# Output projection of a transformer block: six weight parts read during the merge, modulation reads spread between the rows, router on four column groups with a summing product

## What is computed

```python
merged = gates[:, :, 0] * y_pool + gates[:, :, 1] * y_conv + gates[:, :, 2] * y_mla
y = jnp.matmul(merged, w_out)                      # 1024x1024 by 1024x1024
...
h = layer_norm(DEEPNORM_ALPHA * h + y, ln1_g, ln1_b)
...
aff = jax.nn.sigmoid(jnp.matmul(xt, w_router))     # xt is h, w_router is 1024x16
```

## Time and profile before

| | |
|---|---|
| runs | median 3368.93 us of 3 (3367.58 to 3374.35) |
| profiled execution | 3366.2 us, span 3364.5 us |
| busy share of the span | PE 88%, PEld 68%, DVE 61%, ACT 43%, POOL 14% |
| mean granted TensorE clock | 0.936 of full speed |

### The profile page before, as it was taken

How to read it: one execution, slowest core, us unless ns; L and a number is a source line. 1 busy time by engine, 2 the same in 40 slices (tenths; PEclk the granted TensorE clock), 3 DMA queues, 4 the chain that set the end, 5 groups by cost and what they waited for, 6 DMA issues and landing times. The chain is left out here.

```text
span 3364.5 us, 37190 instructions
## 1 busy us (share of the span) xinstructions
PE 2973.2 (88%) x13692; PEld 2296.3 (68%) x13692; DVE 2062.4 (61%) x1983; ACT 1460.3 (43%) x1547; POOL 480.4 (14%) x495
## 2 busy tenths in 40 slices
PE   5999777999997779999997979998988739999994
PEld 3884455666756648888885757886776637888883
DVE  4997464122125668988885634227762268888885
ACT  3112444111102147787764431115651127777773
POOL 0005300000000001111111201009431100000002
PEclk8999899999998889999998989999998769999997
DMA  6112321010106346995224311100012259999995
GB/s 244 47 34 71 124 57 38 35 69 34 69 15 261 126 196 259 392 415 220 80 76 163 111 68 40 48 19 26 1 77 75 115 216 360 392 400 391 401 383 208
DMA packets 113974, 534.57 MB, mean 159 GB/s; under 512 B 15728, under 2 KB 27760, under 8 KB 74048
## 3 DMA queue, kind: packets, MB, share of 16 engines
q1 hardware_dynamic: 91600, 454.07, 35.1%
q0 software_dynamic: 15840, 57.68, 5.2%
q10 hardware_dynamic: 6416, 21.24, 1.7%
HBM read 561.40 MB, written 65.91 MB: 186 GB/s over the span
## 5 line engine op out<-in xcount | busy, mean ns | idle before, releaser
L1763 DVE TENSOR_TENSOR upper_split<-arena,upper_split 128x2048 fp32r<-128x2048 f32 x186 | 415.2, 2286 | 63.3 <-ACT upper_split L1709 63.3
L3081 DVE TENSOR_TENSOR upper_split_experts<-arena,upper_split_experts 128x2048 fp32r<-128x2048 f32 x144 | 328.9, 2292 | 46.0 <-ACT upper_split_experts L3035 44.7
L1709 ACT ACTIVATE upper_split<-arena 128x2048 fp32r<-128x2048 f32 x186 | 342.6, 1914 | 5.2 <-PE banks L177 3.9
L3035 ACT ACTIVATE upper_split_experts<-arena 128x2048 fp32r<-128x2048 f32 x144 | 275.4, 1918 | 95.5 <-PE banks L177 95.5
L175 PE MATMUL banks<-upper_split_experts 128*128 128x512 f32 x768 | 304.1, 396 | 12.4 <-DVE upper_split_experts L3081 12.4
L175 PE MATMUL banks<-upper_split 128*128 128x512 f32 x744 | 296.9, 399 | 11.7 <-DVE upper_split L1763 11.1
L177 PE MATMUL banks<-upper_split_experts 128*128 128x512 f32 x768 | 301.3, 392 | 0.0
L176 PE MATMUL banks<-upper_split_experts 128*128 128x512 f32 x768 | 301.0, 392 | 0.0
L177 PE MATMUL banks<-upper_split 128*128 128x512 f32 x744 | 291.7, 392 | 0.0
L176 PE MATMUL banks<-upper_split 128*128 128x512 f32 x744 | 291.6, 392 | 0.0
L1134 DVE TENSOR_TENSOR upper_latent<-arena,banks 128x512 f32<-128x512 f32 x48 | 33.0, 687 | 340.6 <-PE banks L1079 339.7
(11 more groups left out here) (442 smaller groups left out, 6244.0 us busy)
## 6 DMA issues: line engine op xcount, KB each, us to landing
arena<-in_exp_up_k SPq DMA_DIRECT2D x124, 1024.0 KB
arena<-in_gate_up SPq DMA_DIRECT2D x96, 1024.0 KB, 8.4
arena<-in_exp_down_k SPq DMA_DIRECT2D x62, 1024.0 KB
arena<-in_down SPq DMA_DIRECT2D x48, 1024.0 KB, 7.3
upper_middle<-in_gate_up SPq DMA_DIRECT2D x32, 1024.0 KB, 8.3
upper_middle<-in_down SPq DMA_DIRECT2D x16, 1024.0 KB, 6.9
y<-arena POOLq DMA_DIRECT2D x31, 512.0 KB, 2.9
arena<-in_merge_w SPq DMA_DIRECT2D x8, 1536.0 KB, 7.6
```

The lines of the kernel that those rows point to most:

```text
L1709: a.activation(rounded(high[s]), raw[s], ACT.Copy).then_inc(high_made[up], 1)
L1763: v.tensor_tensor(rounded(low[s]), raw[s], plain(high[s]), ALU.subtract).then_inc(low_made[up], 1)
L3035: a.activation(rounded(high[n % RING]), raw[n % RAW], ACT.Copy).then_inc(high_made, 1)
L3081: v.tensor_tensor(rounded(low[n % RING]), raw[n % RAW], plain(high[n % RING]), ALU.subtract).then_inc(low_made, 1)
```

## The change

In `merge`, SP issues w_out parts 0 to 2 as soon as step 6's gate weights are split and parts 3 to 5 as soon as step 7's are, ahead of the last two stores. Parts 0 to 5 land where `wg` lies, and parts 6 and 7 land behind it, where `merge` keeps its gate values, so these two are issued in the next block. Each part has a buffer of its own. The four vectors are read over parts 0 to 3, each when its part is split. The four pieces of w_ada go out one at a time behind merged(n) and xhat(n) of n = 2 to 5. The router has the operands swapped: 16 columns of its matrix are stationary and 128 columns of `hT` move; part k writes PSUM partitions 32*(k%4) and up, so that eight matmuls make four partial sums (`partial`), ScalarE copies the 128x128 block (`part`), and one product with a constant 0/1 matrix `pick16` adds the four and turns the result (`logits`). VectorE copies all logits once at the end and no longer after each tile.

The diff, cut to its core (left out are the names of semaphores, the placing of `part_of`, and L1356, which now reads `raw[k]`):

```diff
@@ merge, sync
                 for j in range(2):
                     store(it, j)
                     load(it + 1, j)
+            for j in range(2):
+                sp.wait_ge(low_made, (ND - 1 + j) * NB)
+                for k in range(3 * j, 3 * j + 3):
+                    sp.dma_start(m["wo"][k], core.ins["w_out_k"][:, k, :]).then_inc(m["wo_loaded"][k], 16)
             store(last, 0)
             store(last, 1)
@@ output_and_norm
-    raw = [b[n] for n in ("work", "hT", "h0", "h1")]
+    raw = m["wo"]
@@ output_and_norm, sync
-            def load_w(k):
-                if k >= NW:
-                    sp.wait_ge(w_low, k - NW + 1)
-                sp.dma_start(raw[k % NW], core.ins["w_out_k"][:, k, :]).then_inc(wo_loaded[k % NW], 16)
-
             load_merged(0)
-            for k in range(ND):
-                load_w(k)
-                if k == 3:
-                    load_merged(1)
-                    for dst, name in ((ga, "ln_in_g"), (ba, "ln_in_b")):
-                        sp.dma_start(dst, row_on_all(core.ins[name], D)).then_inc(weights, 16)
-                    load_x(0)
-            for dst, name in ((g1, "ln1_g"), (b1, "ln1_b")):
+            for k in range(6, ND):
+                sp.dma_start(raw[k], core.ins["w_out_k"][:, k, :]).then_inc(wo_loaded[k], 16)
+            load_x(0)
+            load_merged(1)
+            load_x(1)
+            sp.dma_start(wr, core.ins["w_router_k"]).then_inc(weights, 16)
+            for i, (dst, name) in enumerate(((ga, "ln_in_g"), (ba, "ln_in_b"), (g1, "ln1_g"), (b1, "ln1_b"))):
+                sp.wait_ge(w_low, i + 1)
                 sp.dma_start(dst, row_on_all(core.ins[name], D)).then_inc(weights, 16)
-            sp.dma_start(wr, core.ins["w_router_k"]).then_inc(weights, 16)
-            load_x(1)
-            for j in range(4):
-                sp.dma_start(m["ada"][j], core.ins["w_ada"][4 + j]).then_inc(ada_loaded, 16)
             for n in range(2, NT):
                 load_merged(n)
                 load_x(n)
+                if n < 6:
+                    sp.dma_start(m["ada"][n - 2], core.ins["w_ada"][n + 2]).then_inc(ada_loaded, 16)
@@ output_and_norm, tensor
-            def logits(n):
+            def partial(n):
                 pe.wait_ge(weights, 16 * 5)
+                pe.wait_ge(cleared, 1)
                 pe.wait_ge(moved, n + 1)
                 if n:
-                    pe.wait_ge(kept, n)
+                    pe.wait_ge(part_moved, n)
                 for k in range(ND):
-                    t = pe.matmul(ps[:, 4, 0:NE], hT[:, k, :], wr[:, k, :], start=(k == 0), stop=(k == ND - 1))
-                t.then_inc(routed, 1)
+                    q = 32 * (k % 4)
+                    t = pe.matmul(ps[q:q + NE, 4, 0:P], wr[:, k, :], hT[:, k, :],
+                                  start=(k < 4), stop=(k >= 4), skip_group_check=True)
+                t.then_inc(parted, 1)
+
+            def logits(n):
+                pe.wait_ge(part_moved, n + 1)
+                pe.matmul(ps[:, 5, n * NE:(n + 1) * NE], part_of, core.col("pick16"),
+                          start=True, stop=True, skip_group_check=True).then_inc(summed, 1)
 
             product(0)
             for n in range(1, NT):
                 product(n)
+                if n >= 3:
+                    logits(n - 3)
                 if n >= 2:
-                    logits(n - 2)
+                    partial(n - 2)
                 turn(n - 1)
+            logits(NT - 3)
+            partial(NT - 2)
+            turn(NT - 1)
             logits(NT - 2)
-            turn(NT - 1)
+            partial(NT - 1)
             logits(NT - 1)
@@ output_and_norm, scalar
+            def part(n):
+                a.wait_ge(parted, n + 1)
+                if n:
+                    a.wait_ge(summed, n)
+                a.activation(part_of, ps[:, 4, 0:P], ACT.Copy).then_inc(part_moved, 1)
+
...
                 a.wait_ge(h_ready, n + 1)
                 a.dma_start(m["h1"][n], b[f"h{n % 2}"]).then_inc(h_stored[n % 2], 16)
+                if n:
+                    part(n - 1)
                 a.wait_ge(turned, n + 1)
-                if n:
-                    a.wait_ge(routed, n)
                 a.activation(b["hT"], flat2(ps, 2), ACT.Copy).then_inc(moved, 1)
+            part(NT - 1)
@@ output_and_norm, vector
-            def keep(n):
-                v.wait_ge(routed, n + 1)
-                v.tensor_copy(m["logits"][:, n * NE:(n + 1) * NE], ps[:, 4, 0:NE]).then_inc(kept, 1)
-
+            v.memset(ps[:, 4, 0:P], 0.0).then_inc(cleared, 1)
...
             for n in range(NT):
                 norm(n)
-                if n:
-                    keep(n - 1)
-            keep(NT - 1)
+            v.wait_ge(summed, NT)
+            c.did(v.tensor_copy(m["logits"], ps[:, 5, 0:P]))
```

More of the change, by code:

```diff
@@ L70, in _columns @@
         ("lams", 4 * HD2), ("c", 8), ("c_ctx", 8), ("zeros", 32),
-        ("eps_rms", 1), ("eps_ln", 1), ("conv2", 12), ("flip", 128),
+        ("eps_rms", 1), ("eps_ln", 1), ("conv2", 12), ("flip", 128), ("pick16", 16),
     ):
@@ L1172, in output_and_norm @@
     sem = lambda n: core.semaphore("og_" + n)
-    NW = 4
     m_loaded, x_loaded, h_stored = ([sem(f"{n}{i}") for i in range(2)] for n in ("m", "x", "h_stored"))
-    wo_loaded = [sem(f"wo{i}") for i in range(NW)]
-    (weights, made, taken, var_ready, rstd_ready, h_ready, turned, moved, routed, kept, steps, pool_steps,
+    wo_loaded = m["wo_loaded"]
+    (weights, made, taken, var_ready, rstd_ready, h_ready, turned, moved, cleared, parted, part_moved, summed, steps, pool_steps,
      ada_loaded, cols_loaded, w_high, w_low, m_high, m_low, scaled) = map(
-        sem, ("weights", "made", "taken", "var", "rstd", "h_ready", "turned", "moved", "routed", "kept", "steps",
+        sem, ("weights", "made", "taken", "var", "rstd", "h_ready", "turned", "moved", "cleared", "parted", "part_moved", "summed", "steps",
               "pool_steps", "ada", "cols", "w_high", "w_low", "m_high", "m_low", "scaled"))
@@ L1186, in output_and_norm @@
     at = m["st_at"]
+    part_of = core.place(at + 32, P)
     st, mv, rstd = core.place(at, 12), core.place(at + 12, 2), core.place(at + 16, 1)
@@ L1299, in high_m @@
                 a.activation(rounded(fl(mh[j])), b[f"mt{j}"], ACT.Copy).then_inc(m_high, 1)
+            def part(n):
[3 more added lines that the diff above has]
+                a.activation(part_of, ps[:, 4, 0:P], ACT.Copy).then_inc(part_moved, 1)
             high_m(0)
             for k in range(ND):
-                a.wait_ge(wo_loaded[k % NW], 16 * (k // NW + 1))
-                a.activation(rounded(wh[:, k, :]), raw[k % NW], ACT.Copy).then_inc(w_high, 1)
+                a.wait_ge(wo_loaded[k], 16)
+                a.activation(rounded(wh[:, k, :]), raw[k], ACT.Copy).then_inc(w_high, 1)
             high_m(1)
@@ L1355, in _ @@
                 v.wait_ge(w_high, k + 1)
-                v.tensor_tensor(rounded(wl[:, k, :]), raw[k % NW], plain(wh[:, k, :]),
-                                ALU.subtract).then_inc(w_low, 1)
+                v.tensor_tensor(rounded(wl[:, k, :]), raw[k], plain(wh[:, k, :]), ALU.subtract).then_inc(w_low, 1)
             low_m(1)
@@ L3244, in build @@
         m["hT_at"], m["free"], m["split"] = at(0), UPPER, m["free"]
+        m["wo"] = [core.place(at(k * D), D) for k in range(ND)]
+        m["wo_loaded"] = [core.semaphore(f"out_w{k}") for k in range(ND)]
         core.open_upper(kind, "upper_split_gates", F32R, m["split"])
@@ L3360, in constants @@
     c["ones"][:] = 1
+    c["pick16"][:] = part[:, None] % 32 == np.arange(NE)[None, :]
     c["before"][:] = part[:, None] < part[None, :]
```

## The result

| | before | after |
|---|---|---|
| median of the runs | 3368.26 us (3364.86 to 3374.35, 4 runs) | 3338.13 us (3337.30 to 3340.84, 4 runs) |
| profiled execution | 3366.2 us, span 3364.5 | 3338.59 us, span 3336.9 |
| from the end of merge's last VectorE instruction to the end of the last copy of logits | 155.3 us | 122.4 us |

The ratio is 0.9911, with a 95% interval from 0.9897 to 0.9926: the kernel is 30 us faster, and the forecast was 3338. That it is met this closely is luck. The output stage gained 32.9 us and not 31.0, and the stages behind it gave 5.3 us back in the profiled execution, which the forecast did not have. So that execution took 3338.6 us where the sum of the prediction gave 3335.2.

A forecast was written before the change was run, and what follows sets the result against it. TensorE, busy in 88% of the span, was taken to bound the kernel, with waits in the output stage. Gains of 25.7 + 4.4 + 0.9 = 31.0 us off 3366.2 gave 3335.2; 2.7 more, a median of 3338, range 3332 to 3346.

The forecast's parts named there:

- The head: Start of the output stage: product(0) no longer waits for w_out parts and ends at 1027.7, before 1034.8; gain 7.1 us.
- it never waits: In product(0), parts 6 and 7 land and all splits finish by 1023.5, while TensorE needs part 7 only at about 1026.
- it costs merge nothing: Parts 0 to 5 read in merge: 7.4 us of transfer, under the 18.19 us of f32 matmuls that close merge.
- The hole: TensorE's 13.62 us wait after product(1) goes, as merged(2) lands earlier; gain 13.8 us, and 1.8 us from the low clock afterwards.
- The router: Router product in column groups: 1.12 us a tile for 1.70, 0.9 for the first; gain 3.1 us by product(7).
- 0.19 a change: In the router, each change of the array's shape costs 0.19 us, twice a tile.
- The tail: After product(7): norm(7) no longer waits for the logits copy, gain 4.4 us; last logits in new form, gain 0.9 us.
- the 2.7 us added for the median: Step from the forecast execution of 3335.2 us to the median of 3338: the median of the runs was 2.7 above the profiled execution.
- The column groups pay: Rival in the router said they don't: 16 instructions in a row, each change in full, 2.3 for 1.12 us; 3346; 11%.
- norm(0) was not late: Rival said it is, before turn(0): vectors or merged(2) land 5 us late, TensorE waits 2 to 4 us; 3343; 10%.
- The later rows: Rival: merged(n+1) waits behind its piece of w_ada; 3377 at 35 us a transfer, decides from about 31; 2%.
- one sign of it: Output stage, tiles 3 to 6: ScalarE waiting for merged would show the prediction wrong; no size given.

## Why the prediction was right, and where a size and a reason were off

*The head, 7.1 us.* product(0) ended at 1027.6 for 1027.7, by the last row of its window, with the splits 1.15 us apart and not 1.27. The size is right and so is the step "it never waits". But the reason given for it, that parts 0 to 5 are read in merge, is not what gives it: with all parts read in the output stage product(1) ended 0.3 us later, so that all but 0.3 of the 7.1 us come from the eight buffers and the unbroken row of reads. Reading in merge does something else, which the prediction did not have: it keeps norm(0) on time, 7.7 us. That it costs merge nothing was right, see the stores above.

*The hole, 13.8 us and 1.8 of clock.* turn(0) began at 1038.48 for 1038.7, and turn(0) with product(2) took 11.86 us at a clock of 1.00, for 11.82. norm(0) was ready at 1036.0 for 1036.2. The run with w_ada in one block shows that this part alone is worth 15.9 us, for the 15.6 of the prediction.

*The router, 3.1 us by product(7).* This term was mis-sized. partial took 0.56 us for 0.9, the summing product 0.22 for 0.21, a steady tile 12.65 for 12.94. The step that failed is "0.19 a change": the row it came from is a change between matmuls of 128 and of 64 rows, and here the two changes together cost 0.14 us. product(7) ended at 1113.3 for 1115.0; 1.5 of these 1.7 us are the router's, the rest was there at turn(0). With the 1.4 us of the tail the new product is worth 6.0 us (the run with the old product and one copy), for the 3.1 and 0.9 of the prediction. "TensorEngine Tiling (Array Packing)" of the Trainium skill, section Key Properties, has a change of tiling mode drain the array; the 0.14 us can be such a drain, but no run shows what they are. "TensorE: Matmul & The Clock Gate", section The mechanism, says that a weight load overlaps running matmuls only if its row group differs. By the prediction's reading that is 0.83 us for four rounds, and the 0.56 us in all contradict it. The same section also has loads into a background weight buffer pulled ahead, which the 0.56 us would allow; no run shows which buffer a load used.

*The tail, 4.4 and 0.9 us.* 13.3 us for 13.5. The two runs with the old product show how it divides: 4.1 us by the copy taken away, 1.4 by the new product.

*What no step had.* The stages behind gave back 2.4 to 5.5 us in three profiles. The forecast for the stage (31.0) was 1.9 too small and the forecast for the rest (nothing) 2.4 to 5.5 too good. For the profiled execution that left the sum 3.4 us too low (3335.2 for 3338.6), and the 2.7 us added for the median, which is a difference of the runs of before and not of these, hid most of it. Run again, the changed kernel has a median of 3334.59 us.

*The rivals.* The column groups pay (one-group run: 6.4 us). norm(0) was not late, but by little: 3 MB more in front of the vectors make it 5.04 us late. The later rows lose nothing behind their piece of w_ada, though one sign of it did come up: ScalarE waited 1.18 us for merged(3), issued at 1029.99 and split at 1041.75. These 11.8 us are more than the 8 of the prediction's sum and far from the 31 at which that rival would decide. For merged(4) to merged(7) ScalarE waited nothing.

## What to carry to other kernels

A large transfer that nobody needs soon belongs behind the small ones that the next step needs, and split up: with the four reads in front the hole was 13.33 us long though they began earlier than before the change, and with them behind it was gone. If a stage begins with transfers, reading some of them in the stage before can be worth more to the engine whose turn comes next than to the one that waits: here 7.7 us against 0.3. A small copy that an engine makes "between" two long steps can hold up the whole chain by waiting in order: collect such results and copy them once.

## What the runs showed of the hardware that was not expected

Changing between 128 and 16 stationary columns in column groups and back costs 0.14 us for the pair by the starts of `partial` (0.19 with what the product and turn around it take more), no more than one change of 0.19 between 128 and 64 rows.

After an idle stretch of over 10 us, TensorE ran at 1.2 GHz for 4.0 us in the changed kernel and for 5.7 us when it began 1.2 us earlier, so an earlier start need not be an earlier end. In the run with one column group the wait before the last turn was 1.23 us, behind a `partial` of 1.91 us, and turn ran at full clock (1.09 us for the eight transposes); in the changed kernel the wait was 3.80 us, behind a `partial` of 0.63 us, and turn took 1.97. The faster turn made up for the longer `partial` behind it.

The same instructions in the differential attention took from 264.6 to 267.8 us over the fourteen profiles, and 267.3, 267.4 and 265.8 in three of one kernel. The granted clock of the last 28 us was 0.94 in six of them (267.3 us and more) and 1.00 in the others. The instructions that differ between these kernels lie some 1,100 us earlier.
